# A weight pipeline with two slots for raw units instead of three, and seven half slots for split weights instead of six

## The reference

```python
for i in range(DEPTH):                       # block 1
    h = rms_norm(x, ln_attn_g[i])
    dq, dk, dv, mq, mk, mv = jnp.split(h @ w_in[i], cuts, axis=-1)
    ...
    x = x + jnp.concatenate([y_diff, y_moba], axis=-1) @ w_out[i]
    x = x + conv_ffn(rms_norm(x, ln_ffn_g[i]), w_up[i], conv_w[i], conv_b[i], w_down[i])
...
for l in range(DEPTH):                       # block 2
    x = x + 0.5 * swiglu(rms_norm_2(x, ffn1_norm[l]), ffn1_w_gate[l], ffn1_w_up[l], ffn1_w_down[l])
    h = rms_norm_2(x, mix_norm[l])
    proj = h @ w_in[l] + b_in[l]
    ...
    y_attn = forgetting_attention(q, k, v, log_f) @ w_o_attn[l]
    yr = rg_lru(xr, ...) * jax.nn.gelu(gr)
    y_rnn = yr @ w_o_rnn[l]
    merged = jax.nn.sigmoid(g_attn) * y_attn + jax.nn.sigmoid(g_rnn) * y_rnn
    x = x + merged @ w_out[l]
    x = x + 0.5 * swiglu(rms_norm_2(x, ffn2_norm[l]), ffn2_w_gate[l], ffn2_w_up[l], ffn2_w_down[l])
```

## Time and profile before

| what | value |
|---|---|
| median of 3 runs | 1952.39 us (1950.72 to 1953.18) |
| profiled execution, time | 1950.9 us |
| its span, first to last instruction | 1949.1 us |
| mean granted clock of TensorE | 0.988 of full speed |
| PE busy | 97% of the span |
| DVE busy | 62% |
| ACT busy | 57% |
| DMA traffic | 340.83 MB, mean 175 GB/s |

### The profile page before, as it was taken

How to read it: one execution, slowest core, us unless ns; L and a number is a source line. 1 busy time by engine, 2 the same in 40 slices (tenths; PEclk the granted TensorE clock), 3 DMA queues, 4 the chain that set the end, 5 groups by cost and what they waited for, 6 DMA issues and landing times.

```text
span 1949.1 us, 23235 instructions
## 1 busy us (share of the span) xinstructions
PE 1896.1 (97%) x9146; PEld 1579.8 (81%) x9146; DVE 1204.6 (62%) x1746; ACT 1110.5 (57%) x1594; POOL 41.6 (2%) x60
## 2 busy tenths in 40 slices
PE   6989999999999999989999999999998999999999
PEld 4868888877888788878888888888888887888888
DVE  5767767676777655437875654555454597655544
ACT  5757555776555544448865454454443787645442
POOL 2000000000000000000020100000000002000000
PEclk8999999999999999989999999999998999999999
DMA  7444555436555555534465655545554446455553
GB/s 250 151 130 152 175 208 179 148 117 200 190 187 177 173 192 178 192 106 139 164 236 180 219 176 194 194 153 201 188 185 138 138 145 226 165 183 193 180 188 107
DMA packets 157207, 340.83 MB, mean 175 GB/s; under 512 B 5942, under 2 KB 18715, under 8 KB 156587
## 3 DMA queue, kind: packets, MB, share of 16 engines
q1 hardware_dynamic: 153920, 327.57, 50.2%
q0 software_dynamic: 2720, 11.58, 1.8%
q10 hardware_dynamic: 459, 0.20, 0.0%
HBM read 338.24 MB, written 1.09 MB: 174 GB/s over the span
## 4 chain that ended last, share of the span: by engine, by line
PE 86%; DVE 5%; ACT 5%; DMA 2%; issue 1%; SPq 0%; ACTq 0%; DVEq 0%
PE bank L430 27%; PE bank L432 26%; PE bank L431 26%; DVE w_lo L1653 2%; DMA raw<-in_w_in 2%; ACT w_hi L1066 1%; PE bank L589 1%; PE bank L543 1%; DMA raw<-in_ffn_w_gate 1%; DVE r_lo L1682 1%; PE bank L497 1%; PE bank L654 1%; PE bank L675 1%; PE bank L631 1%; PE bank L719 1%
## 5 line engine op out<-in xcount | busy, mean ns | idle before, releaser
L1653 DVE TENSOR_TENSOR w_lo<-raw,w_hi 128x1024 fp32r<-128x1024 f32 x620 | 736.1, 1224 | 336.9 <-ACT w_hi L1066 330.2
L1066 ACT ACTIVATE w_hi<-raw 128x1024 fp32r<-128x1024 f32 x620 | 636.3, 1057 | 341.7 <-PE bank L432 312.2
L430 PE MATMUL bank<-w_hi,r_hi 128*128 128x512 f32 (+1 forms) x1792 | 688.9, 384 | 18.2 <-DVE par L1933 9.0
L432 PE MATMUL bank<-w_hi,r_lo 128*128 128x512 f32 (+1 forms) x1792 | 680.3, 380 | 0.0
L431 PE MATMUL bank<-w_lo,r_hi 128*128 128x512 f32 (+1 forms) x1792 | 679.7, 379 | 0.0
L430 PEld LDWEIGHTS bank<-w_hi,r_hi 128*128 128x128 f32 x1792 | 339.1, 189 | 84.0 <-DVE par L1933 10.3
L432 PEld LDWEIGHTS bank<-w_hi,r_lo 128*128 128x128 f32 x1792 | 338.7, 189 | 63.9
L431 PEld LDWEIGHTS bank<-w_lo,r_hi 128*128 128x128 f32 x1792 | 339.2, 189 | 61.0
L430 PE MATMUL bank<-w_hi,z_hi 128*128 128x512 f32 x656 | 260.2, 397 | 2.0 <-DVE z_lo L1653 2.0
L432 PE MATMUL bank<-w_hi,z_lo 128*128 128x512 f32 x656 | 256.1, 390 | 0.0
L431 PE MATMUL bank<-w_lo,z_hi 128*128 128x512 f32 x656 | 255.4, 389 | 0.0
(11 more groups left out here) (204 smaller groups left out, 1403.6 us busy)
## 6 DMA issues: line engine op xcount, KB each, us to landing
raw<-in_w_in SPq DMA_DIRECT2D x80, 1024.0 KB, 5.1
raw<-in_w_up SPq DMA_DIRECT2D x44, 1024.0 KB, 5.2
raw<-in_ffn_w_gate SPq DMA_DIRECT2D x44, 1024.0 KB, 5.0
raw<-in_ffn_w_up SPq DMA_DIRECT2D x44, 1024.0 KB, 5.1
raw<-in_ffn_w_down SPq DMA_DIRECT2D x44, 1024.0 KB, 4.9
raw<-in_w_down SPq DMA_DIRECT2D x22, 1024.0 KB, 5.0
raw<-in_w_out SPq DMA_DIRECT2D x16, 1024.0 KB, 5.1
raw<-in_w_o_rnn SPq DMA_DIRECT2D x8, 1024.0 KB, 6.3
```

Source lines behind the costliest of these rows:

```text
L430: pe.matmul(out_, lh, rh, start=start, stop=False, skip_group_check=True)
L432: return pe.matmul(out_, ll, rh, start=False, stop=stop, skip_group_check=True)
L1066: A_(w_hi[:, n % NH, :], raw[:, u % NS, HALF * h:HALF * (h + 1)], ACT.Copy).then_inc(hi_ready, 1)
L1653: return V.tensor_tensor(dst, src, hi.bitcast(F32), ALU.subtract)
```

## The change

Two constants change. `raw` gets two slots of 8 KB a partition instead of three; `w_hi` and `w_lo` get seven half slots instead of six, 4 KB a partition each. The memory in use stays the same.

```diff
--- before
+++ after
@@ -23,8 +23,8 @@
 CW = 512
 STEPS = 6
 HALF = UNIT // 2
-NS = 3
-NH = 6
+NS = 2
+NH = 7
 EPS = 1e-6
 NEG = -1e30
 BUCKETS = 32
```

## The result

The changed kernel takes 2036.3 us (median of 4 runs, 2034.48 to 2041.51) against 1951.66 us for the kernel before in the same session. The ratio is 1.0437, 95% interval 1.0417 to 1.0458, so it is slower by 84.6 us. 2016 us was predicted, with a range of 1974 to 2047. The profiled execution took 2036.09 us, its span is 2034.3 us, and the mean granted clock is 0.973 instead of 0.988.

The account below looks back on a forecast made before the run. TensorE was taken as the bound, busy 1896.1 of 1949.1 us, with little margin in attention and mixers. Terms 9.4 + 18.3 + 19.7 + 3.8 + 10.1 + 2.3 = 63.6 us on 1950.9 gave 2014.5, 2016 as median; range 1974 to 2047.

Parts of the forecast that it names:

- the signs: PE's expected waits in each mixer: before v's copy, 18 to 20 us; before the last z_lo, 10 and 2 us.
- Start, 0: Program start: unit 2's load leaves later, but PE has two other units to work on first; 0 us.
- Block 1, 4.7 a layer: Block 1's attention stage: w10's late load delays the turned probabilities' copy PE takes at once; 9.4 us over two layers.
- FFNs, 0: FFN stages: late loads are eaten within the step, since ACT waits for PE there anyway; 0 us.
- Mixer up to m21, 18.3 and 19.7: Middle of block 2's mixers: late loads add up on ACT until v's copy delays PE; 18.3 us layer 0, 19.7 layer 1.
- a stall is eaten where ACT already waits: Counting rule for all stages: ACT's existing waits absorb load lateness, which goes on where ACT is full; no size itself.
- Behind it, 1.9 a layer: Mixers after m21: m24's load meets three POOL transfers, making the turned probabilities' copy late for PE; 3.8 us in all.
- End, 10.1 and 2.3: Mixer ends: m39's late load delays the last z_lo; 10.1 us in layer 0 beside POOL's loads, 2.3 in layer 1.
- rival 4: More: the convolution's late loads hit a copy PE waits for, or long stalls cost PE clock; 2046 us, chance 0.08.
- No change (1): Whole kernel: two slots suffice on average and the split weights' lead makes late loads good; 1951 to 1956 us, chance 0.09.
- Less (2): Stalls are real, but ACT's order has more slack or POOL's transfers miss m39's load; 29 us, 1981 us, chance 0.18.
- Faster (3): ACT's wait for PE shrinks, and a tenth of PE's idle time goes; 5 us gained, 1947 us, chance 0.03.

Follow-up runs that it names:

- the extra matmuls: Changed kernel plus 17 unused matmuls before w8's chunk, 10 before the turned probabilities ahead of m26, 36 and 6 before w_out's third unit; 2029.14 us, ratio 1.0401.
- the first of the two kernels with extra matmuls: Changed kernel plus 11, 22, 14 unused matmuls before turned copies of chunks 1, 3, 5 in both mixers, 34 before w_out's third unit in layer 0; 2031.16 us.

## Why the prediction was right, and where it was not

**The mechanism held in the main, 21 us short, and the largest term is in part luck.** Loads that leave later, ACT held up by them at fixed places of its list, PE late by that: this is what the trace and the split by stages show. Where PE feels it was wrong: it stands still in seven places of mixer 0 (m5, m10, m15, m20, m23, m26, m38) where the signs named two, and not before v's copy. The 21 us that are missing are 0.9 at the start, 5.7 in block 1, 3.8 in the mixers up to m21, 8.5 behind it and 2.1 at the ends. In the order of its steps:

- *Start, 0.* 0.9 us in this trace, 0.4 and 0.7 in two others. Kernels whose first loads leave as before show up to 0.4, and the one with late loads in block 1 shows 0.0, so it can't be told from 0.
- *Block 1, 4.7 a layer.* The lateness of ACT at w10 came out nearly right: 5.4 forecast, 6.0 in the trace (80.97 against 73.93, less the 1.0 that ACT was late already at w6). The way there left out w7, whose load by the prediction's own numbers lands at 61.5 (56.4 and 5.1) where ACT wanted it at 57.43, and for which ACT waits 4.11 us. The place where PE feels it was wrong, and the size with it. I took the copy of turned probabilities at 96.54 as the first thing that PE takes at once. But `store(2, ...)` (line 1312) stands behind w9's and w10's high parts, and PE waits for it ahead of w8's chunk, at 82.75. PE stands 4.4 us there. Nothing of the seventh half slot helps, and some 1.5 us of clock follow, which the extra matmuls gave back in both layers.
- *FFNs, 0.* Right, in the trace to 0.3 us and by the kernel with late loads there alone (+0.6, interval -1.0 to +2.3). That rests on one step read and held for all.
- *Mixer up to m21, 18.3 and 19.7.* 20.7 and 21.1. The sum is near, but the step that gives it failed: "a stall is eaten where ACT already waits", and PE delayed only where v's copy is. PE is stopped four times before and behind m16 (m5, m10, m15, m20), each time by a copy or a store that stands behind a late high part. m5's stall has its cause in m6's load (ACT waits 5.08 us for it), which my list of loads passed over. The two ways of counting agree here only because in this kernel ACT's lateness grows from stall to stall and hardly any of it is eaten, so the near hit is luck in part. With m12's load alone they differ, 5 against 14 to 16, and 19.1 was measured.
- *Behind it, 1.9 a layer.* This term was mis-sized: 6.2. m24's load took 10.9 us as forecast, and the copy of turned probabilities was late by it (m23 1.6). No run takes the POOL transfers away there. But m26's and m27's loads hold up the exponentials of the third pair, m26's low parts stand before its row maxima on DVE, and PE waits 2.86 us for the scaled probabilities. I had stopped reading at m24.
- *End, 10.1 and 2.3.* 12.2 and 2.3. The load took 12.4 us (12.8 forecast), the stall 9.54, and 2.5 us of clock came behind it. Both the meeting of transfers and the clock were taken away singly, and each took its share of the time with it (9.7 us, and 2.6 in the trace).

**The clock was rival 4's and belonged in the sum.** The prediction put it at nothing without a reason. PE's busy time grew by 23.9 us. That is no measure of what clock cost, as the first of the two kernels with extra matmuls shows: what PE loses to the clock between two stalls of one chain is swallowed by the second. Where nothing follows, it counts. Five such places (w8 twice, m26 twice, the end of mixer 0) gave back 7.2 us, so about a third of the 21 us that were missing. The other two thirds are in the main stalls of loads that the list passed over (w7's, m6's, m26's); they weren't priced one by one.

**The rivals.** No change (1): refuted outside the FFNs. Less (2): its argument, that the order has more slack than I count, fails for m12, and its other, that m39's load doesn't meet the side loads, fails by the landing time. Faster (3): refuted, ACT's waits for PE did shrink to 51.8 us, and it gained nothing. More (4): its FFN half fell, its clock half held.

What stays open: how much of the clock's loss in the middle of the mixers counts, since in the first kernel with extra matmuls layer 0 got back nothing there and layer 1 3.5 us.

## What to carry to other kernels

How deep a buffer must be isn't told by the mean rate, but by the time from release to landing against the shortest stretch between two uses in the list of the engine that waits; then look at what stands behind that wait on the same engine, for that is what the bound engine feels. A stall of the bounding engine wasn't given back in any trace here, even if the engine that caused it catches up: find the places where it takes something at once, and price each. If memory is short, try a ring of halves: here it gave back half of the loss for one more issue a unit.

## What the runs showed of the hardware

- Stalls of TensorE as short as 2.2 us in the middle of dense work (at 1020.76) were followed by matmuls 0.43 to 0.57 us apart instead of 0.23, and 1.3 to 2.8 us were lost behind such a stall. Where extra matmuls filled the gap (w8, m26, the end of mixer 0), that loss was gone.
- It isn't sure to happen at that length. At the end of mixer 1 of the changed kernel PE stood 2.13 us, and its matmuls were soon 0.23 apart:

```profile
1831.56 0.50 PE L430 MATMUL bank<-w_hi,z_hi 128*128 128x512 f32 x1 [2.13 <-DVE z_lo L1653]
1831.90 0.39 PE L431 MATMUL bank<-w_lo,z_hi 128*128 128x512 f32 x1
1832.13 0.39 PE L432 MATMUL bank<-w_hi,z_lo 128*128 128x512 f32 x1
```

- A load of 1 MB that lands in 5.0 us without them took 12.4 us beside five transfers of POOL with 2 MB in all. At m12 a load of 0.5 MB landed in 3.5 us where one of 1 MB took 5.0; over all loads the medians are 4.4 to 4.6 and 5.1.
